# The operand tiles of a two-block transformer kernel begin 96 bytes later in on-chip memory, the weight rings stay

## The reference

```python
u    = _rmsnorm(h, norm_mix_w);  proj = u @ w_in                   # q k v z beta dec | q k v | gates
mix  = sigmoid(gate_a) * (y_a @ w_branch_gdn) + sigmoid(gate_b) * (y_b @ w_branch_moba)
h    = h + mix @ w_out
u    = _rmsnorm(h, norm_ffn_w)
h    = h + (silu(u @ w_ffn_gate) * (u @ w_ffn_up)) @ w_ffn_down
...
proj = h @ a_w_in                # q, k, v, g of the differential layer; then @ a_w_out, layer norm
kvf  = hk @ kv_w                 # k, v, forget logits
proj = h @ b_w_in                # q, g of the forgetting layer; then @ b_w_out, layer norm
```

## Time and profile before

| what | value |
|---|---|
| median of 3 runs | 2553.62 us (2551.00 to 2556.72) |
| profiled execution, its own time | 2552.91 us |
| profiled execution, span | 2551.1 us |
| granted TensorE clock, mean | 0.996 |
| TensorE busy | 2503.7 us, 98% of the span |
| VectorE / ScalarE busy | 1805.3 us / 1151.4 us |
| moved by DMA | 605.71 MB, 237 GB/s over the span |

### The profile page before, as it was taken

One profiled execution on the slowest core, in us unless ns is written; L12 is line 12 of the kernel. 1 busy time (PEld: TensorE's weight loads), 2 busy tenths in 40 slices (PEclk: granted clock), 3 DMA queues, 4 the chain that ended last, 5 costly groups with the idle time before them and its releaser, 6 DMA issues.

```text
span 2551.1 us, 38207 instructions
## 1 busy us (share of the span) xinstructions
PE 2503.7 (98%) x14496; PEld 2135.8 (84%) x14496; DVE 1805.3 (71%) x2342; ACT 1151.4 (45%) x1445; POOL 0.2 (0%) x4
## 2 busy tenths in 40 slices
PE   8999999999999999999999999999999999999998
PEld 8987878778888888888888888899987778999886
DVE  6897676776667777777776767777786665556666
ACT  5544333355544544444443334444496344434642
POOL 0000000000000000000000000000000000000000
PEclk9999999999999999999999999999999999999999
DMA  7777676786768888888887777888845556675464
GB/s 215 240 250 254 211 256 217 257 258 207 261 222 275 273 282 280 281 284 279 280 279 257 259 259 259 288 285 291 268 141 184 190 166 187 186 238 176 138 222 141
DMA packets 317515, 605.71 MB, mean 237 GB/s; under 512 B 27310, under 2 KB 31412, under 8 KB 315708
## 3 DMA queue, kind: packets, MB, share of 16 engines
q1 hardware_dynamic: 301628, 571.59, 69.3%
q10 hardware_dynamic: 15744, 32.15, 3.6%
HBM read 593.03 MB, written 10.62 MB: 237 GB/s over the span
## 4 chain that ended last, share of the span: by engine, by line
PE 90%; DVE 5%; DMA 2%; ACT 2%; issue 1%; SPq 0%; ACTq 0%; DVEq 0%
PE bank L666 22%; PE bank L668 22%; PE bank L667 22%; PE bank L692 5%; PE bank L691 5%; PE bank L693 5%; PE bank L609 2%; DMA gemv_w<-in_w_mod 1%; PE bank L796 1%; DVE w_lo L1937 1%; DVE gemv_acc L1956 1%; DVE conv_out L2085 1%; ACT w_hi L1290 1%; PE bank L1129 1%; PE bank L822 0%
## 5 line engine op out<-in xcount | busy, mean ns | idle before, releaser
L1937 DVE TENSOR_TENSOR w_lo<-raw,w_hi 128x1024 fp32r<-128x1024 f32 x820 | 1001.2, 1223 | 656.6 <-ACT w_hi L1290 653.9
L1290 ACT CAST w_hi<-raw 128x1024 fp32r<-128x1024 f32 x820 | 859.9, 1050 | 1299.2 <-PE bank L668 974.2
L666 PE MATMUL bank<-w_hi,u_hi 128*128 128x512 f32 x1216 | 487.0, 401 | 3.8 <-DVE w_lo L1937 3.7
L668 PE MATMUL bank<-w_hi,u_lo 128*128 128x512 f32 x1216 | 478.4, 393 | 0.0
L667 PE MATMUL bank<-w_lo,u_hi 128*128 128x512 f32 x1216 | 476.1, 392 | 0.0
L1956 DVE SCALAR_TENSOR_TENSOR gemv_acc<-gemv_w,small,gemv_acc 128x512 f32<-128x512 f32 x480 | 358.0, 746 | 42.8 <-DMA gemv_w<-in_w_mod 26.3
L666 PE MATMUL bank<-w_hi,s_hi 128*128 128x512 f32 x744 | 297.6, 400 | 1.8 <-DVE w_lo L1937 1.5
L668 PE MATMUL bank<-w_hi,s_lo 128*128 128x512 f32 x744 | 292.8, 394 | 0.0
L667 PE MATMUL bank<-w_lo,s_hi 128*128 128x512 f32 x744 | 291.1, 391 | 0.0
L691 PE MATMUL bank<-s_hi,w_hi 128*128 128x256 f32 x1024 | 285.1, 278 | 0.0
L692 PE MATMUL bank<-s_lo,w_hi 128*128 128x256 f32 x1024 | 285.0, 278 | 0.0
(11 more groups left out here) (364 smaller groups left out, 2863.4 us busy)
## 6 DMA issues: line engine op xcount, KB each, us to landing
gemv_w<-in_w_mod SPq DMA_DIRECT2D x384, 256.0 KB, 3.2
raw<-in_w_in SPq DMA_DIRECT2D x176, 512.0 KB, 4.5
raw<-in_a_w_in SPq DMA_DIRECT2D x128, 512.0 KB, 4.7
raw<-in_w_ffn_gate SPq DMA_DIRECT2D x88, 512.0 KB, 4.6
raw<-in_w_ffn_up SPq DMA_DIRECT2D x88, 512.0 KB, 4.4
raw<-in_w_ffn_down SPq DMA_DIRECT2D x88, 512.0 KB, 4.3
gemv_w<-in_kv_w_mod SPq DMA_DIRECT2D x128, 256.0 KB, 3.9
raw<-in_kv_w SPq DMA_DIRECT2D x64, 512.0 KB, 3.7
```

The source lines that it names most:

```text
L666: pe.matmul(o, xh, w_hi[:, s, t], start=(k == 0), stop=False)
L668: ins = pe.matmul(o, xl, w_hi[:, s, t], start=False, stop=(k == 2 * units - 1))
L1290: act.copy(w_hi[:, s], raw[:, s]).then_inc(hi_done, 1)
L1937: dve.tensor_tensor(w_lo[:, s], raw[:, s], w_hi[:, s].bitcast(F32), ALU.subtract).then_inc(lo_done, 1)
```

## The change

One constant is added, and the region begins that many bytes later. Its slots keep their distances from one another, and the rings and everything else ahead of the region keep their places.

```diff
+OPERANDS_AT = 96
...
-        region = at[0]
+        region = at[0] + OPERANDS_AT
```

## The result

| | median | runs |
|---|---|---|
| before | 2554.73 us | 4, 2551.00 to 2556.72 |
| changed | 2583.20 us | 4, 2581.19 to 2588.18 |

The ratio is 1.0116, with a 95% interval from 1.0097 to 1.0135. The profiled execution of the changed kernel took 2584.03 us, its span is 2582.2 us, 31.1 us more than before.

The account below looks back on a forecast made before the run. The prediction took TensorE, busy 98% of the span, to bound the kernel. From 2552.9 us, -17.3 and -9.2 (two other terms 0) gave 2526.4 us, 1.0% faster; the range leaving out at most 2 in 10 was 2492 to 2584 us.

Parts of the forecast that it names:

- terms 3 and 4: VectorE and ScalarE reads of operand tiles, and weight transfers with waits for `w_lo`: each taken as 0.
- Term 1: 512-column form, 2592 triples in all stages: pace gets faster, -17.3 us.
- one step down: Assumed pace change of the 512-column form, to 6: -17.3 us over 2592 triples.
- The worst case that I counted: Both matmul forms slower: 17.3 + 18.4 = 36 us lost, upper end of the slower times, 2589 us.
- The large gain: Gain beyond one or two steps of the 512-column form, below 2505 us; chance 0.10.
- Term 2: 256-column form, 1408 triples: all go at the fast pace, -9.2 us; called the weaker term.
- The slower rival: Region now begins at a multiple of 32, not 64, so the kernel slows to 2562 to 2589 us; chance 0.28.
- the pieces: Extra cost for operands not beginning at a multiple of 64 bytes, whatever the distance: 28.2 us lost.
- The rival of no effect: TensorE's surcharge comes from the order of loads and passes, not from places: 2553 us; chance 0.24.

Follow-up runs that it names:

- e1_all96: Against the kernel before: rings and operand region all begin 96 bytes later, their distance staying 192; 2552.70 us, ratio 0.9994.
- e4_region128: Against the kernel before: operand region begins 128 bytes later, rings stay, distance 320 modulo 512; 2588.37 us, ratio 1.0133.
- e9_sweep: Separate kernel, not the reference computation: series of 24 equal matmuls, stationary operand moved in 16-byte steps against the moving one; ran once, no whole-kernel time given.
- e2_region64: Against the kernel before: operand region begins 64 bytes later, rings stay, distance 256; 2554.95 us, ratio 1.0006.
- e11_part64: Against the kernel before: only the operands of `w_out`, `ffn` and `down` (and `mod_rows` behind them) begin 64 bytes later; 2546.45 us, ratio 0.9973.
- e6_dist352: Against the kernel before: operand region begins 160 bytes later, rings stay, distance 352 modulo 512; ratio 1.0185.

## Why the prediction was wrong

**That the change works through TensorE's pace alone: right.** Nothing on another engine changed by more than 2.1 us of busy time, and terms 3 and 4 of the sum were right at 0. The time from the last matmul to the end is 12.7 us in the changed kernel, 12.8 before.

**That the distance between ring and region sets it: right, and shown.** e1_all96 keeps the distance and the time; e4_region128 keeps the alignment and loses 1.3%; e9_sweep finds the same paces with nothing else running. I had the span of the distance as 512 bytes; it is 256. In e9_sweep bfloat16 with 512 columns goes at 215.8 to 215.9 ns at the four distances tried, and float32r (128 stationary columns) takes at least 10.8 ns more at every distance measured.

**Term 1, the step that failed.** I took "one step down" for the 512-column form, -17.3 us, which is 6.67 ns on each of 2592 triples. The step was an assumption of mine, and so was the "6" that it leads to: no run shows this form in steps of 6.67 ns. By distance its triple takes 681.7, 687.3 or 697.5 to 702.7 ns, and the change took it from 687.3 to 699.8, 12.5 ns up. The other paces in the trace of before belonged to another form, so they said nothing on what this form does at another distance. 687.3 ns was not high for it: 697 to 703 is what it takes at most distances, and 192 was its second best. That gives 2592 x 12.5 = +32.4 us, of which `spill` absorbed 6.4. The worst case that I counted, both forms a step worse, had +17.3 us for this form, too low by a factor of two for the same reason. The large gain, from which the lower end of my range (2492 us) was reckoned, is not shown by any run either: the best distance measured is worth 14.8 us to this form.

**Term 2: right only that both forms move.** I took the fast pace for all 1408 triples, -9.2 us; measured was 350.4 ns, which is 1408 x 3.7 = +5.2 us, and `qkv`, where the triple went from 353.0 to 350.8 ns before 106 us and from 340.1 to 353.4 ns between 120 and 153 us, changed its length by 0.1 us. The reason I gave, that what helps one form helps the other, is refuted by e2_region64: the best distance for 512 columns (681.7) is a worst for 256 (360.0).

**The slower rival: the right time for the wrong reason.** Its 28.2 us ("the pieces") give 2581 us, and 2583 was measured. They are 6.67 ns on each of the 4224 matmuls of the 256-column form, 20.0 ns per triple, for operands off a multiple of 64 bytes, and nothing on the 512-column form; no run shows such a cost. The 256-column triple grew by 3.7 ns, the loss lies in the 512-column form, and e1_all96, all at odd multiples of 32, loses nothing. A time alone would have confirmed it.

**The rival of no effect** had for it that the 256-column pace flips with all places fixed. The flip is real, but it is no rival to the distance. It has two paces at four of the eight distances, and both of them go with the distance: 340.0 and 353.3 ns at 192, 350.0 and 353.3 at 32, 356.0 and 360.0 at 128, 352.0 and 356.0 at 160. And the 512-column form, which carries the loss, goes at 699 to 700 ns in every large stage of the changed kernel.

**The size of the whole.** 26.0 us from the 2080 triples outside `spill`, and 5.1 - 0.8 from the two layers' 256-column products, give 30.3 us; the spans differ by 31.1.

What stays open: why the distance matters. e9_sweep shows that of the three types float32r alone has it (the other two at the four distances tried), that other engines and DMA are not needed, and that it does not shrink in proportion to the stationary columns (a spread of 7.4 ns with 32 of them, of 6.2 with 128). The last speaks against the picture that the pass is disturbed by the load of the next weights, in proportion to what is loaded. What picks one of the two paces is open too: at the distance of the kernel before, the sweep's series stayed at 117.8 ns and never showed 113.3.

## What to carry to other kernels

Where TensorE bounds a float32r kernel, as here with 98% of the span, the place of its operands relative to one another is a tuning parameter worth 2% here (2546.45 us with e11_part64, 2600.92 with e6_dist352), and it must be tried per matmul shape, since the best distance for one shape (681.7 ns for the 512-column triple at 256) was a worst for another (360.0 for the 256-column one). A start-to-start distance over a few hundred equal matmuls resolves it to a tenth of a nanosecond, where the total can hide two effects of opposite sign (e2_region64). And a buffer added or moved anywhere between rings and operands changes that distance: before an edit is blamed or credited for a per cent, compare the paces.

## What was not expected of the hardware

- Three float32r matmuls of 128x128 by 512 columns take from 681.7 to 702.7 ns on average in this kernel, by the distance of the operands modulo 256 bytes; in e9_sweep bfloat16 and float32 show no such effect at 0, 32, 64 and 128 (215.8 to 215.9 ns, 429.2 ns per record).
- At distance 192 the 256-column form has two steady paces, 340.0 and 353.3 ns for three. It flips after an interruption and keeps the new pace for over 150 us; a kernel with all its tiles moved by 96 bytes has the same two in the same layers. At 32, 128 and 160 there are two as well, 3.3 to 4.0 ns apart.
- Float32r matmuls with a stationary operand of 32 columns are not always faster than those with 128: at distances 0 and 32 they are slower (231.7 against 227.3 ns, 238.0 against 233.2), at 64 and 128 faster (231.7 against 233.4, 230.7 against 233.4), and at 160 equal.
